# Four value products gathered into one block behind the fourth turned probabilities

## The reference, cut to what matters

```
xn = rmsnorm(x, pre_mix_g[l]);  proj = xn @ w_in[l]
gate_a, gate_b = sigmoid(proj[..., s5:s6]), sigmoid(proj[..., s6:])
y_a = rglru_branch(...) @ w_pa[l]                 # z @ w_pa
y_b = swa_sink_attention(...) @ w_pb[l]           # o @ w_pb
mixed = (gate_a * y_a + gate_b * y_b) @ w_o[l]
x = x + rmsnorm(mixed, post_mix_g[l])
x = x + rmsnorm((silu(h @ w_gate) * (h @ w_up)) @ w_down, post_ffn_g[l])   # h = rmsnorm(x)
```

```
p = softmax([s, sink])[..., :-1]        # per chunk c: 64 queries x 128 keys x 16 heads
o = p @ v                               # the "value product" of the chunk
```

## Time and profile before

| | us |
|---|---|
| median of 3 runs | 805.85 (805.75 to 806.32) |
| the profiled execution's own time | 806.01 |
| its span, first to last instruction | 804.2 |
| PE busy in the span | 793.4 |
| DVE busy | 601.7 |
| ACT busy | 460.2 |

### The profile page before, as it was taken

The page is one execution under the profiler, slowest core; times in us unless marked ns, Lnnn a source line. Parts: engine busy times, 40 slices in busy tenths (PEclk is TensorE's granted clock), DMA queues, the critical chain, the costliest instruction groups (busy, mean ns, idle before and its releaser), DMA issues.

```text
span 804.2 us, 10534 instructions
## 1 busy us (share of the span) xinstructions
PE 793.4 (99%) x4250; PEld 666.9 (83%) x4250; DVE 601.7 (75%) x602; ACT 460.2 (57%) x591; POOL 76.4 (9%) x135
## 2 busy tenths in 40 slices
PE   7999999999999999999999999999999999999997
PEld 5897898888888888888889889988888888888885
DVE  6799897647689878667489869965567896985762
ACT  5568976643456555535455788865436555465341
POOL 3830000000120000000011200000003100000000
PEclk9999999999999999999999999999999999999999
DMA  9857444445388786862476735434654869768501
GB/s 292 259 208 248 147 139 153 147 168 209 111 307 233 224 309 176 261 213 102 157 225 222 260 129 185 158 108 155 222 196 146 277 184 293 211 223 262 209 0 53
DMA packets 84276, 156.48 MB, mean 195 GB/s; under 512 B 7314, under 2 KB 27906, under 8 KB 84228
## 3 DMA queue, kind: packets, MB, share of 16 engines
q1 hardware_dynamic: 80000, 147.42, 53.6%
q0 software_dynamic: 4224, 8.39, 6.0%
q10 hardware_dynamic: 4, 0.00, 0.0%
HBM read 154.75 MB, written 1.05 MB: 194 GB/s over the span
## 4 chain that ended last, share of the span: by engine, by line
PE 93%; issue 2%; DMA 2%; ACT 1%; DVE 1%; POOL 0%; DVEq 0%; POOLq 0%; ACTq 0%
PE work L771 13%; PE work L773 13%; PE work L772 13%; PE acc L771 9%; PE acc L773 9%; PE acc L772 9%; PE work L763 4%; PE work L764 4%; PE work L765 4%; PE work L857 3%; PE work L858 3%; PE work L859 3%; DMA lru_a<-in_w_ffn_gate 1%; PE work L960 1%; PE acc L885 1%
## 5 line engine op out<-in xcount | busy, mean ns | idle before, releaser
L1532 DVE TENSOR_TENSOR weights_lo<-weights_raw,weights_hi 128x2048 fp32r<-128x2048 f32 x114 | 260.4, 2289 | 88.8 <-ACT weights_hi L1145 88.6
L1145 ACT ACTIVATE weights_hi<-weights_raw 128x2048 fp32r<-128x2048 f32 x116 | 221.6, 1915 | 160.9 <-PE work L773 83.4
L771 PE MATMUL work<-weights_hi,act_a_hi 128*128 128x512 f32 x416 | 164.2, 395 | 0.0
L773 PE MATMUL work<-weights_hi,act_a_lo 128*128 128x512 f32 x416 | 162.4, 390 | 0.0
L772 PE MATMUL work<-weights_lo,act_a_hi 128*128 128x512 f32 x416 | 162.0, 389 | 0.0
L771 PE MATMUL acc<-weights_hi,act_b_hi 128*128 128x512 f32 x240 | 94.8, 395 | 0.0
L773 PE MATMUL acc<-weights_hi,act_b_lo 128*128 128x512 f32 x240 | 93.7, 390 | 0.0
L772 PE MATMUL acc<-weights_lo,act_b_hi 128*128 128x512 f32 x240 | 93.5, 390 | 0.0
L773 PEld LDWEIGHTS work<-weights_hi,act_a_lo 128*128 128x128 f32 x416 | 78.1, 188 | 16.6
L771 PEld LDWEIGHTS work<-weights_hi,act_a_hi 128*128 128x128 f32 x416 | 78.2, 188 | 16.3 <-issue 0.8
L772 PEld LDWEIGHTS work<-weights_lo,act_a_hi 128*128 128x128 f32 x416 | 78.2, 188 | 15.7
(11 more groups left out here) (216 smaller groups left out, 1259.7 us busy)
## 6 DMA issues: line engine op xcount, KB each, us to landing
weights_raw<-in_w_in SPq DMA_DIRECT2D x43, 1024.0 KB, 5.1
weights_raw<-in_w_ffn_gate SPq DMA_DIRECT2D x16, 1024.0 KB, 7.4
weights_raw<-in_w_ffn_up SPq DMA_DIRECT2D x12, 1024.0 KB, 5.7
weights_raw<-in_w_ffn_down SPq DMA_DIRECT2D x12, 1024.0 KB, 4.7
weights_raw<-in_w_pa SPq DMA_DIRECT2D x8, 1024.0 KB, 4.9
weights_raw<-in_w_pb SPq DMA_DIRECT2D x8, 1024.0 KB, 4.9
weights_raw<-in_w_o SPq DMA_DIRECT2D x8, 1024.0 KB, 4.8
q_feat<-in_w_ffn_down SPq DMA_DIRECT2D x6, 1024.0 KB, 8.5
```

The costliest lines, as they stand in the source:

```text
L771: mm(dst, xh, wh, start=first, stop=False)
L773: return mm(dst, xl, wh, start=False, stop=final)
L1145: activate(w_hi[:, SLOT[n], :], raw_slot(RAWS[n]), ACT.Copy).then_inc(hi_done.sem, 1)
L1532: v.tensor_tensor(w_lo[:, SLOT[n], :], raw_slot(RAWS[n]), bits(w_hi[:, SLOT[n], :]), ALU.subtract).then_inc(split_done.sem, 1)
```

## The change

In each layer:

- PE: the four value products stand in one block, behind `turn_p(3)`, and this block stands between the two pa pairs. Products 0 and 1 no longer stand ahead of pa 0, and `turn_p(3)` no longer stands between panels pa 0 and pa 1.
- Products 0 and 1 are written to acc banks 0 and 1 and wait for the last scores to have been read (`score_read` 8). Their two entries leave the list of work banks, in which all others keep their banks.
- `prob_t(2)` is the second half of AG and `prob_t(3)` is KTOK, so that `p_copy(2)` and `p_copy(3)` no longer wait for value products 0 and 1 to have read UC.
- On ACT `p_copy(3)` stands ahead of the split of pb 0, and the four high parts of `o` behind it; on DVE the four low parts stand behind the split of pb 0.

```diff
-    uses = [(use, k % 4) for k, use in enumerate(uses)]
+    uses = [(use, k % 4) for k, use in enumerate(uses) if use not in (("pv", 0), ("pv", 1))]
...
         def prob_t(c):
-            return UC[:, 4 * (c % 2):4 * (c % 2) + 4, :].rearrange("p a (h k) -> p (a h) k", h=2)
+            if c == 3:
+                return KTOK[:, :, :, :].rearrange("p t g k -> p (t g) k")
+            half = UC[:, 4 * c:4 * c + 4, :] if c < 2 else AG[:, 4:8, :]
+            return half.rearrange("p a (h k) -> p (a h) k", h=2)
...
+            if name == "pv" and n < 2:
+                return acc[:, n, :]
...
                 def pv_product(c):
-                    dst = claim(l, "pv", c)
+                    if c < 2:
+                        dst = bank("pv", c)
+                        pe.wait_ge(*score_read.at(l, 8))
+                    else:
+                        dst = claim(l, "pv", c)
...
-                pv_product(0)
-                pv_product(1)
                 pe.wait_ge(*z_lo_done.at(l, 4))
-                t_pair("pa", 0, z_hi, z_lo, between=lambda: turn_p(3))
-                pv_product(2)
-                pv_product(3)
+                t_pair("pa", 0, z_hi, z_lo)
+                turn_p(3)
+                for c in range(NC):
+                    pv_product(c)
                 t_pair("pa", 1, z_hi, z_lo)
...
                 def p_copy(c):
-                    act.wait_ge(*(h_done.at(l, 2) if c < 2 else pv.at(l, c - 1)))
+                    if c < 2:
+                        act.wait_ge(*h_done.at(l, 2))
...
-                    if (name, j) == ("gate_b", 3):
-                        o_hi_part(0)
-                        o_hi_part(1)
+                    if (name, j) == ("pa", 1):
+                        p_copy(3)
...
-                    if (name, j) == ("pa", 0):
-                        p_copy(3)
                     if (name, j) == ("pa", 1):
-                        o_hi_part(2)
-                    if (name, j) == ("pa", 2):
-                        o_hi_part(3)
+                        for c in range(NC):
+                            o_hi_part(c)
```

More of the change, by code:

```diff
@@ L2069, in layer @@
                         z_lo_part(3)
-                    if (name, j) == ("gate_b", 3):
-                        o_lo_part(0)
-                        o_lo_part(1)
                     if (name, j) == ("pa", 1):
-                        o_lo_part(2)
-                    if (name, j) == ("pa", 2):
-                        o_lo_part(3)
+                        for c in range(NC):
+                            o_lo_part(c)
                     if (name, j) == ("pb", 1):
```

## The result

The median went from 805.9 us to 808.62 us (7 runs of each, 808.15 to 808.98 after). The ratio is 1.0029, with a 95% interval of 1.0019 to 1.0038: slower, by 2.7 us where 2.3 were forecast. The profiled execution has a span of 807.0 us against 804.2 before.

A forecast was written before the change was run, and what follows sets the result against it. PE was taken to bound the kernel, busy 793.4 of 804.2 us. Per layer -0.64 - 0.885 - 0.03 + 2.70 = +1.15 us, +2.3 for two layers, gave 808.15 us, with an 8 in 10 range of 807.2 to 808.9.

The forecast's parts named there:

- The first stretch: From gate_b's last matmul to pa's second: 1.91 us instead of 2.55, as pa 0 waits for both tanhs.
- the release: Time from the tanhs' end at 545.20 to pa 0's start at about 545.26, taken from DVE's release at 662.78.
- The restart: From pa 0's first to its second matmul after the wait: 0.33 us where a running stream has 0.227.
- The pair without the transposes: Panels pa 0 and pa 1 without turn_p(3) between them: 0.885 us less, and some 0.03 for slower matmuls behind a switch.
- The block behind it: turn_p(3) and 64 value matmuls between the two pa pairs: 5.25 us, 2.70 more than before, free of waits.
- The inner switch: From turn_p(3)'s transposes to value matmuls inside the block: 0.09 us extra, with 0 and 0.2 as bounds.
- Sum by causes: Per layer: +1.35 idle, +0.10 restart, -0.20 and -0.12 for switches; the sum by parts is +1.15 us.
- The wait: Ahead of pa 0, for both tanhs: +1.35 us idle and +0.10 restart a layer.
- The gathering itself: Switches saved per layer: 0.20 us around the first value block and 0.12 around turn_p(3).
- The clock: Rival: PE's clock falls at each new gap, 2.5 us twice, about 813 us; chance 0.03.
- further wait: Rival: product 3 or the second pa pair waits too; 1 us a layer gives 810.2; chance 0.05.
- The rival of no wait: Rival: pa 0 starts without waiting or waits briefly; only switches left, -0.6 us, 805.2; chance within 0.2%: 0.12.

The follow-up runs named there:

- e1: Changed kernel with work banks 0 and 1 swapped for 2 and 3 for all uses from pa 0 to turn_m 3; 805.28 us.
- e3: Changed kernel with pa 1's bank claimed only ahead of its own tile, so pa 0 waits for one tanh, not two; 807.64 us.
- e7: Changed kernel with value product 0 alone put back ahead of pa 0, the other three behind turn_p(3); 806.63 us.
- e4: Changed kernel with turn_p(3) back between pa 0 and pa 1, the four value products still in one block behind the pair; 808.67 us.
- e5: Changed kernel with PE's wait for pa 0's weights ahead of the two claims, not behind them; 808.40 us, one run.
- e6: Changed kernel with four more, long-passed waits behind the claims of the pa pair; 808.46 us, one run.

## Why the prediction was right

**The first stretch: right in kind, 0.16 us too small.** The step was that the value products had covered the two tanhs and that pa 0 would wait for both. It does (e1, e3, e7). From gate_b's last matmul to pa's second it said 1.91 us; it is 546.89 - 544.82 = 2.07. The mis-sized term is the release. I took 0.06 us from DVE's release at 662 us; here 546.59 - 546.34 = 0.25 us pass after the tanhs' end. The restart was 0.30 instead of 0.33.

**The pair without the transposes: right.** From its second to its last matmul the forecast has 46 steps of 0.227, 10.44 us, and the trace 557.36 - 546.89 = 10.47.

**The block behind it: 5.25 forecast, 562.54 - 557.36 = 5.18 measured,** with two errors that nearly cancel. The inner switch costs 0.18 and not 0.09, still inside its bounds. And 64 value matmuls take 3.64 us in one block (e4; 562.21 - 558.56 = 3.65 in the kernel after), not 2 x 1.90. Inside the block 32 of them take 1.79 to 1.80 and 16 take 0.87 to 0.88; only the last 16 take 0.97 to 0.98, so some 0.1 us of each 1.90 belongs to leaving a block and is paid once. That the block came out so close is in part luck.

**Sum by causes.** The wait costs 1.65 us a layer (after against e1), where 1.45 was said. The gathering itself gives 0.41 (e1 against before), where 0.30 was said, and all of it comes from one block of value matmuls instead of two; `turn_p(3)`, for which 0.12 was said, gives 0.01 (after against e4). 1.65 - 0.41 = 1.24 us, where 1.15 was said: a wait 0.20 us longer than forecast, less 0.11 more of gain.

**From 2.49 to 2.7.** Two layers of the stretch are 2.49 us; the medians differ by 2.7, the spans by 2.8. In the two profiled spans the waits at the feed-forward part add 0.22 (layer 0) and 0.37 (layer 1), and the kernel after came to its first gate_b end 0.34 us sooner. Both scatter from run to run, and the interval of the ratio (1.5 to 3.1 us) holds 2.49.

**The rivals.** The clock did not fall: the granted clock is 1.00 from 149 to 152 and from 544 to 547 us, and the matmuls behind the gaps keep their pace, 0.30 us for the first and 0.23 from then on. The pace is the safer sign. The granted clock also reads 1.00 from 7 to 10 us in the kernel before, where the transposes took twice their later time; it does react at the end of the kernel after, 0.74 over the span's last 6 us, where PE has run out of work. In its table of why this matters for your kernels the Trainium skill ("TensorE: Matmul & The Clock Gate") warns of idle gaps longer than these, so it neither spoke against this change nor is tested by it. No further wait appeared: `p_copy(3)` ended at 559.31 and product 3 started at 561.23, 1.9 us of cover as worked out, and the last low part of `o` was ready at 565.84, 7.4 us ahead of pb at 573.22. The rival of no wait is what e1 made true, at 805.28 where -0.6 us had been forecast for it (805.2). One sum in its paragraph is off: with 1.1 us of idle time, 0.10 of restart and 0.30 of switches saved, a layer would have come to 0.9 and not 0.8 us, 1.8 in all, so the sign turns doubtful only below about 1.0 us. That moves nothing in the forecast.

## What to carry to other kernels

Where small work stands between two large streams on the bounding engine, ask what other engine is finishing under it before moving it: here 1.9 us of value products hid 1.1 us of tanhs that free the next banks, which end 1.5 us behind the start of the last large matmul. Gathering the small work was worth 0.4 us a layer, and it pays only once the next stream claims buffers that were freed earlier; changing the order and the round of banks together turned a loss of 2.7 us into a gain of 0.8. Work that covers a wait is free only up to the end of that wait: the first of the two products, put back into the gap, took 0.87 us off the stretch (17.72 - 16.85), nearly its whole length; the second took off only 0.39 (16.85 - 16.46).

## What the runs showed of the hardware beyond that

- A release reached PE after 0.06 us where DVE gave it and after 0.25 us where ACT's second tanh gave it, with two claims and a passed wait in between (the kernel after). With the passed wait ahead of the claims the gap was 0.11 us shorter (e5, one run), but four more waits did not lengthen it (-0.05, e6, one run). Why is open.
- A switch of kind on PE has no single price: 0.01 us from large matmuls into transposes, 0.09 into value matmuls, 0.18 from transposes into these (the kernel after against e4).
- A load of 1 MB in the same place of the program took between 10.07 and 10.57 us in eight profiles, and its scatter reached PE one for one.
